# Hybrid RWKV-7 / Mamba-2 / short-convolution block: the first round's norm and logits inside the opening strips, and the key shift ahead of a split

## The reference, cut to what matters

```python
h = rmsnorm(x, norm_w[l]);  p = h @ w_in[l]            # 256 x 2048 times 2048 x (some 17,500)
pa = token_shift(pa, mu)                               # p + mu * (prev - p)
r, k, v, g, dw, da = jnp.split(pa, [...])
log_w = -softplus(-(w0 + tanh(dw) @ w2)) - 0.5         # decay logits: rank 64
decay = exp(-exp(log_w));  a = sigmoid(a0 + da @ a2)   # a second rank 64 product
kk = k * k_k;  k = k * (1.0 + (a - 1.0) * k_a)
kh = kk / maximum(sqrt(sum(kk * kk, axis=-1)), 1e-12)  # norm over each head of 64
# state-space branch: per head, over 256 tokens
dt = softplus(dt + dt_bias);  a_cs = cumsum(dt * a)    # "acs" in the kernel
seg = exp(a_cs[l] - a_cs[s]) where l >= s
```

## Time and profile before

| | |
|---|---|
| median of 3 runs | 1207.26 us (1206.23 to 1207.36) |
| the profiled execution | 1207.42 us |
| its span, first to last instruction | 1205.7 us |
| mean granted TensorE clock | 0.995 of full speed |
| PE busy | 1173.4 us (97%) |
| PEld busy | 1041.9 us (86%) |
| DVE busy | 798.7 us (66%) |
| ACT busy | 572.9 us (48%) |
| POOL busy | 67.8 us (6%) |

### The profile page before, as it was taken

How to read it: one execution, slowest core, us unless ns; L and a number is a source line. 1 busy time by engine, 2 the same in 40 slices (tenths; PEclk the granted TensorE clock), 3 DMA queues, 4 the chain that set the end, 5 groups by cost and what they waited for, 6 DMA issues and landing times.

```text
span 1205.7 us, 23555 instructions
## 1 busy us (share of the span) xinstructions
PE 1173.4 (97%) x8502; PEld 1041.9 (86%) x8502; DVE 798.7 (66%) x1174; ACT 572.9 (48%) x828; POOL 67.8 (6%) x94
## 2 busy tenths in 40 slices
PE   6998999999999999999999999999999999999996
PEld 5997999999899998998989988888888888888885
DVE  4776769678686786876968765754555565546553
ACT  5454446455364554544535444543544444445442
POOL 2001001010010110100101002000000000000000
PEclk9998999999999999999999999999999999999999
DMA  6755635546455354553555536466666666658662
GB/s 167 210 158 132 172 106 158 136 120 172 121 156 153 105 159 137 150 156 104 158 135 139 161 111 204 140 211 208 193 192 190 196 196 193 189 184 283 194 195 95
DMA packets 254747, 197.24 MB, mean 164 GB/s; under 512 B 23943, under 2 KB 207472, under 8 KB 254064
## 3 DMA queue, kind: packets, MB, share of 16 engines
q1 hardware_dynamic: 252228, 195.82, 56.3%
q10 hardware_dynamic: 2476, 0.84, 0.3%
HBM read 193.71 MB, written 2.11 MB: 162 GB/s over the span
## 4 chain that ended last, share of the span: by engine, by line
PE 93%; ACT 2%; DVE 2%; issue 1%; DMA 1%; POOL 0%; SPq 0%; DVEq 0%; ACTq 0%
PE ps L1163 15%; PE ps L1164 13%; PE ps L1165 13%; PE ps L1241 11%; PE ps L1242 11%; PE ps L1243 11%; PE ps L1489 2%; PE ps L1490 2%; PE ps L1491 2%; PE ps L1275 1%; ACT whi L427 1%; PE ps L1358 1%; PE ps L1350 1%; PE ps L1371 1%; DMA o<-in_x 1%
## 5 line engine op out<-in xcount | busy, mean ns | idle before, releaser
L724 DVE TENSOR_TENSOR wlo<-raw,whi 128x1024 fp32r<-128x1024 f32 (+1 forms) x356 | 437.1, 1241 | 241.4 <-ACT whi L427 239.8
L427 ACT ACTIVATE whi<-raw 128x1024 fp32r<-128x1024 f32 (+1 forms) x356 | 372.8, 1054 | 308.4 <-PE ps L1243 182.1
L1163 PE MATMUL ps<-hhi,whi 128*128 128x256 f32 (+1 forms) x1440 | 422.1, 293 | 0.2 <-DVE wlo L724 0.2
L1164 PE MATMUL ps<-hlo,whi 128*128 128x256 f32 (+1 forms) x1440 | 407.4, 283 | 0.0
L1165 PE MATMUL ps<-hhi,wlo 128*128 128x256 f32 (+1 forms) x1440 | 407.2, 283 | 0.0
L1163 PEld LDWEIGHTS ps<-hhi,whi 128*128 128x128 f32 (+1 forms) x1440 | 274.2, 190 | 16.8 <-issue 13.4
L1164 PEld LDWEIGHTS ps<-hlo,whi 128*128 128x128 f32 (+1 forms) x1440 | 274.7, 191 | 0.7
L1165 PEld LDWEIGHTS ps<-hhi,wlo 128*128 128x128 f32 (+1 forms) x1440 | 274.4, 191 | 0.3
L1241 PE MATMUL ps<-whi,hhi 128*128 128x512 f32 x384 | 151.3, 394 | 0.0
L1243 PE MATMUL ps<-whi,hlo 128*128 128x512 f32 x384 | 149.6, 390 | 0.0
L1242 PE MATMUL ps<-wlo,hhi 128*128 128x512 f32 x384 | 149.5, 389 | 0.0
(11 more groups left out here) (270 smaller groups left out, 1137.4 us busy)
## 6 DMA issues: line engine op xcount, KB each, us to landing
raw<-in_w_in SPq DMA_DIRECT2D x548, 256.0 KB, 3.1
raw<-in_w_branch SPq DMA_DIRECT2D x96, 256.0 KB, 3.7
raw<-in_w_out SPq DMA_DIRECT2D x64, 256.0 KB, 3.6
o<-in_x SPq DMA_DIRECT2D x4, 1024.0 KB, 6.8
acb<-acs_rows SPq DMA_DIRECT2D x8, 256.0 KB, 3.4
out_y<-lots SPq DMA_DIRECT2D x3, 512.0 KB, 4.6
lots<-in_final_norm_w SPq DMA_DIRECT2D x1, 1024.0 KB, 10.2
lots<-ad SPq DMA_DIRECT2D x32, 8.0 KB
```

Source lines behind the costliest of these rows:

```text
L427: sc.activation(whi[:, slot, :, 0:width], raw[:, slot, :, 0:width], ACT.Copy).then_inc(hi_done, 1)
L724: tt(wlo[:, slot, :, 0:width], raw[:, slot, :, 0:width], whi[:, slot, :, 0:width].bitcast(F32), ALU.subtract).then_inc(lo_done, 1)
L1163: mm(dst, a, khi, start=first, stop=False)
L1164: mm(dst, a, klo, start=False, stop=False)
```

## The change

- **TensorE:** the transposes of the decay rows and time steps and `norm_and_logits(0)` move from behind the opening into it, after chunk 25. The transposes go to bank `E` instead of `B`, and TensorE no longer waits for ScalarE's copy before the norm.
- **VectorE:** `shift_k(0)` and `shift(0, 0)` move in front of the split in step c = 25 (chunk 27's); `kk_floor(0)`, `kk_recip(0)` and `decays(0)` in front of the split in step c = 27 (chunk 29's).
- **ScalarE:** the copy `dat` follows the split in step c = 26. In step c = 27, in front of the split, it waits for the store of the decay rows, issues their first load itself, and does `kk_root(0)` and `half_logits(0)`.
- **SyncE:** the wait for that store and the first load of the decay rows are gone.
- **Loop, VectorE:** `shift_k(j + 1)` moves from t = 32, behind that step's split, to t = 31, in front of it.

The definitions of the helpers move up with their first use and are the same; they are left out of the diff here.

```diff
@@ SyncE @@
-            sp.wait_ge(s["acs_st"], 16)
-            load_acs(0)
             with sp.Fori(0, CT - 1) as j:
                 main(j, False)
@@ ScalarE @@
             for c in range(PRE):
                 n = c + AHEAD
+                if c == 27:
+
+                    act.wait_ge(s["acs_st"], 16)
+                    act.dma_start(acb[:].rearrange("p e t -> p (e t)"), acs_d[0:1, :].broadcast_to([P, 2 * T])
+                                  ).then_inc(s["acb_in"], 16)
+                    kk_root(0)
+                    half_logits(0)
                 if n > 2:
                     split_hi(n, n % RING, n // RING + 1, P + 16 if n < 4 else CW, first=n < RING)
+                if c == 26:
+                    act.wait_ge(s["dt_tr"], 1)
+                    sc.activation(dat[:].rearrange("p w b h -> p (w b h)"), E[:, 0:64], ACT.Copy).then_inc(s["dat_ok"], 1)
                 if c == 4:
...
-            act.wait_ge(s["dt_tr"], 1)
-            sc.activation(dat[:].rearrange("p w b h -> p (w b h)"), B[:, 0:64], ACT.Copy).then_inc(s["dat_ok"], 1)
...
-            kk_root(0)
-            half_logits(0)
@@ VectorE @@
             for c in range(PRE):
                 n = c + AHEAD
+                if c == 25:
+                    shift_k(0)
+                    shift(0, 0)
+                if c == 27:
+                    kk_floor(0)
+                    kk_recip(0)
+                    decays(0)
                 if n > 2:
                     split_lo(n, n % RING, P + 16 if n < 4 else CW)
...
-            shift_k(0)
-            shift(0, 0)
-            kk_floor(0)
-            kk_recip(0)
-            decays(0)
...
-                    if t == 32 and not last:
+                    if t == 31 and not last:
                         shift_k(j + 1)
@@ TensorE @@
-            pe.wait_ge(s["acs_ok"], 1)
-            pe.wait_ge(s["scm_ok"], 4)
-            for w, src in enumerate((acs[:], dts[:, 5, :])):
-                for b in range(2):
-                    op = tr(B[:, (2 * w + b) * 16:(2 * w + b + 1) * 16], src[:, b * P:(b + 1) * P], ident[0:16, 0:16])
-            op.then_inc(s["dt_tr"], 1)
-            pe.wait_ge(s["dat_ok"], 1)
-            pe.wait_ge(s["lr_ok"], 1)
-            pe.wait_ge(s["const_o"], 1)
...
+                if c == 25:
+
+                    pe.wait_ge(s["acs_ok"], 1)
+                    pe.wait_ge(s["scm_ok"], 4)
+                    for w, src in enumerate((acs[:], dts[:, 5, :])):
+                        for b in range(2):
+                            op = tr(E[:, (2 * w + b) * 16:(2 * w + b + 1) * 16], src[:, b * P:(b + 1) * P], ident[0:16, 0:16])
+                    op.then_inc(s["dt_tr"], 1)
+                    pe.wait_ge(s["lr_ok"], 1)
+                    pe.wait_ge(s["const_o"], 1)
+                    norm_and_logits(0)
...
-            norm_and_logits(0)
```

More of the change, by code:

```diff
@@ L454, in _, with kk_root, half_logits @@
             act.wait_ge(s["prm_d"], 1)
+            def kk_root(j):
+                act.wait_ge(s["kk_max"], j + 1)
+                sc.activation(knrm, ksq, ACT.Sqrt).then_inc(s["kk_rt"], 1)
+            def half_logits(j):
+                act.wait_ge(s["lora_mm"], j + 1)
+                sc.activation(tanhs[:, 0, :], A[:, 0:T], ACT.Tanh, scale=0.5, bias=halfb[:, bass.ds(j, 1)])
+                sc.activation(tanhs[:, 1, :], C[:, 0:T], ACT.Tanh, scale=0.5,
+                              bias=halfb[:, bass.ds(j + CT, 1)]).then_inc(s["tanh_wa"], 1)
             for c in range(PRE):
                 n = c + AHEAD
+                if c == 27:
[4 more added lines that the diff above has]
+                    half_logits(0)
                 if n > 2:
                     split_hi(n, n % RING, n // RING + 1, P + 16 if n < 4 else CW, first=n < RING)
+                if c == 26:
+                    act.wait_ge(s["dt_tr"], 1)
+                    sc.activation(dat[:].rearrange("p w b h -> p (w b h)"), E[:, 0:64], ACT.Copy).then_inc(s["dat_ok"], 1)
                 if c == 4:
@@ L749, in _, with shift, shift_k, kk_floor @@
             ts(dskh[:], dsk[:], 0.5, None, ALU.mult).then_inc(s["prm_d"], 1)
+            def shift(j, w):
+                dve.wait_ge(tile_out, PRE_TILES + j * ITER_TILES - 3 + ORDER[w])
+                stt(sh[:, w, :], pq[:, w, 0:T], prm[:, bass.ds(j + (MU + w * CT), 1)], qq[:, w, :], ALU.mult, ALU.add
+                    ).then_inc(s["shifted"], 1)
+            def shift_k(j):
+                shift(j, 1)
+                dve.wait_ge(s["shifted"], j * 4 + 1)
+                ts(kk, sh[:, 1, :], prm[:, bass.ds(j + KK, 1)], None, ALU.mult).then_inc(s["kk_ok"], 1)
+            def kk_floor(j):
+                dve.wait_ge(s["kk_mm"], j + 1)
+                ts(ksq, B[:, 0:T], 1e-24, None, ALU.max).then_inc(s["kk_max"], 1)
+            def kk_recip(j):
+                dve.wait_ge(s["kk_rt"], j + 1)
+                v.reciprocal(krin, knrm).then_inc(s["kk_rin"], 1)
+            def decays(j):
+                dve.wait_ge(s["tanh_wa"], j + 1)
+                ts(sga, tanhs, 0.5, 0.5, ALU.mult, ALU.add).then_inc(s["sig_wa"], 1)
+                dve.wait_ge(s["sig_wa"], j + 1)
+                v.tensor_tensor_scan(ls, restart[:], sga[:, 0, :], 0.0, ALU.mult, ALU.add).then_inc(s["cum"], 1)
             for c in range(PRE):
                 n = c + AHEAD
+                if c == 25:
[5 more added lines that the diff above has]
+                    decays(0)
                 if n > 2:
@@ L794, in _ @@
                         tt(scm[:, g, :], ps[:, 4 + g, 0:384], causal[:], ALU.mult).then_inc(s["scm_ok"], 1)
[L796 to L822, removed]
             def gate_split(n, i, y):
@@ L1178, in half_chunk, with norm_and_logits @@
                     op.then_inc(chunk_used, 1)
+            def norm_and_logits(j):
+                pe.wait_ge(s["kk_sq"], j + 1)
+                mm(B[:, 0:T], head1[:], ksq, start=True, stop=True).then_inc(s["kk_mm"], 1)
+                pe.wait_ge(lora_in, j * 32 + 32)
+                mm(A[:, 0:T], lorat[0:64, 0, :], lr[0:64, :], start=True, stop=True)
+                mm(C[:, 0:T], lorat[64:128, 1, :], lr[64:128, :], start=True, stop=True).then_inc(s["lora_mm"], 1)
             x_by_channel(0, 8)
```

## The result

The changed kernel takes 1192.2 us (median of 4 runs, 1191.8 to 1193.5) against 1207.06 us before: a ratio of 0.988, 95% interval 0.9863 to 0.9897, that is 14.9 us or 1.2% less. Forecast were 1193.9 us and a range of 1192.8 to 1197.8. A second timing, with a later set of runs, gave 1192.6 against 1207.7 (0.9876, 0.9861 to 0.9891).

A forecast was written before the change was run, and what follows sets the result against it. TensorE, busy 97%, was taken as the bound, with time to win only in its waits and low clock. Opening 7.6 plus loop 5.8 made 13.4 us, giving 1193.9 us; own range 1192.9 to 1195.2, 8-in-10 range 1192.8 to 1197.8.

The forecast's parts named there:

- The opening, 7.6 us: Norm and logits inside the opening's strips: shorter idle wait 3.7, norm at full clock 1.0, faster round 1 2.9 us.
- the stop: TensorE's 3.88 us idle wait before the first norm, for GpSimd's square of the keys; falls to 0.2, gain 3.7 us.
- the cold norm: First norm to round 1's first product: 2.27 us at low clock, 1.26 at full clock, gain 1.0 us.
- the wait I kept for the square: Opening: TensorE's new wait for GpSimd's square of the keys, 0 to 0.5 us, taken as 0.2.
- The first round: Round 1's excess of 2.90 us over round 2, from half clock and waits at lines 1320 and 1292, all goes.
- The chain to the keys: Opening, norm to scaled keys on VectorE: done at 110.7 us, 1.3 us before TensorE needs them at 112.0.
- I count nothing for it: SyncE's loads of chunks 28 and 29, no longer behind the store's wait: in time even unmoved, so no gain.
- if it is late after all, at least the clock's 1.6 comes back: Round 1: should the scaled keys be late, 1.6 us of the 2.9 us gain still comes from the clock.
- The loop, 7 x 0.83 = 5.8 us: Key shift in front of the split in seven rounds: TensorE's wait at the norm goes, 0.83 us a round.
- VectorE's 0.90 us keeps the distance: Loop: all VectorE's later work moves forward by 0.90 us, so the chain to the next scaled keys keeps its distance.
- The late opening chain: First rival: floor, root, tanh and decays over 1.3 us later than summed, round 1 keeps its waits; 1195.2 to 1197, chance 0.12.
- the second one: Second rival: GpSimd's square goes first, VectorE's split waits 0.61 us each round, loop worth 2.0 us; 1197.7, chance 0.09.

## Why the prediction was right in kind and too small

**The opening, 7.6 us: right in sum.** The first products of the two executions start 0.28 us apart (17.55 and 17.83). With that, the norm of round 2 comes 181.41 - 173.24 + 0.28 = 8.45 us earlier, 0.86 of it its own stall: 7.6. By its terms: the stop and the cold norm give 4.9 instead of 4.7, because the wait I kept for the square, 0.2, was none. The first round gives 2.7 instead of 2.9: I had all of line 1320's wait go, and 0.4 us stayed (24.78 against 24.38), since it depends on the small transfers too. The chain to the keys was summed to within 0.1 us, and the run with the norm a chunk later confirms its room.

**SyncE, "I count nothing for it": wrong, and hidden by the sum.** Put back, wait and load cost 3 us; alone in the old order their removal gives 3.6. I checked whether chunk 28 would be in time for TensorE. I should have asked what else stands behind its split on ScalarE. The sum held by luck: I had laid out the head of round 1 as if nothing held ScalarE there, which is true only with this edit. A fallback of mine fails as well, "if it is late after all, at least the clock's 1.6 comes back": in the run with the loop's edit alone the clock came back early and the keys took the time, and with the load alone on ScalarE the clock fell later instead.

**The loop, 7 x 0.83 = 5.8 us: the step that failed.** I bounded a round's gain by the stall, "between the counted 0.70 and the full 0.98 - 0.12 = 0.86". It is mis-sized: a round gives 0.97, the term 6.8. With the transfers out of the way a round falls from 77.27 to 76.30, 0.97 us. The stall is 0.86 of it. The other 0.11 is the restart: a norm whose square is already there takes 1.16 us to the next product, one that was waited for 1.26 (1.15 to 1.16 and 1.26 to 1.27 in every round from the second on). The weights of the norm itself point at the cause, weights that are not loaded ahead through a stop: they are loaded 0.12 us ahead of it where nothing is waited for (173.12 and 173.24 above), and only with it behind a stop, in the kernel before:

```profile
181.41 0.30 PEld L1212 LDWEIGHTS ps<-lots,head 128*128 128x128 f32 x2 [0.90 <-POOL lots L366]
```

7 x 0.97 = 6.8, and the loop's edit alone measured 6.8. The sentence that VectorE's 0.90 us keeps the distance held, and mattered: without it 0.4 us of each round goes back.

**What was in no term: about 0.6 us.** The waits at line 1320 of rounds 2 to 7, up to 0.2 us each, were not seen as waits, since the list of waits shows only that of round 1. They depend on when the small transfers land: with these first, they are gone in both orders. "Late" fell from 0.72 to 0.14 between the two profiles, and 7.6 + 6.8 + 0.6 makes 15.0. In the six profiles of kernels with the changed opening and the old order of transfers it runs from 0.03 to 0.70, so whether the change lowers it for a reason or by chance is left open. With the small transfers first in both kernels the change is worth 1205.07 - 1191.18 = 13.9 us; by the medians about 1 us of the 14.9 depends on when these transfers land.

**The rivals.** The late opening chain did not come (1.5 us of room), nor did the second one: in the loop the split went first. In the opening GpSimd went first and VectorE's splits lost 0.4 us, inside the room. The Trainium skill (SBUF — State Buffer, "Who interferes with whom") has it that the two share one pair of ports under an exclusive lock, and that the order of issue decides who blocks. The trace agrees to within 0.15 us, with both orders in the changed kernel. In the loop the split had 1.06 of its 1.22 us left when the square started, and the square took 1.53 us, 0.92 more than alone. In the opening the square had 0.55 us left when the splits started, and they took 2.77 us, 0.43 more than alone. The range was too narrow below: its lower end took 0.5 for the runs, 0.2 for the opening's wait and 7 x 0.03 for the loop off the forecast, with no allowance for a term larger than the stall.

## What to carry to other kernels

A stop of the bounding engine costs more than its idle time: the first instructions behind it are not prepared, 0.1 us each time here, and the clock was half from the norm on for 5.6 us behind the stop of 3.88 us, and for some 3 us behind that of 2.33. What the clock gives back counts only where nothing else is late. When work moves past a queue's wait, ask of every in-order engine what stands behind the instruction that is held, not only whether the held one is in time. A list that shows a wait once may hide a smaller one in every round; comparing the same distance from round to round finds it.

## What the runs showed of the hardware

With small transfers (8 KB) issued behind 512 KB of weights on the same queue, the work that waits for them started with a spread of 0.25 us from round to round (the solve, 10.64 to 10.89 us after the transposes in rounds 2 to 7 of the kernel before), and with them issued in front with none that could be seen (10.10 us in each of the same rounds). Behind stops of TensorE of 3.88 and 2.33 us the granted clock was 0.50 for a time, and behind those of 1.3 us and less it stayed at 1.00 (the run with load and wait on SyncE, and that with the norm after chunk 26). How long it stays low varies: 3.5 us from the norm on in the run with the loop's edit alone, 5.6 in the kernel before, with the same opening. ScalarE's table load took 1.28 us and the instruction behind it started at its end (99.76 + 1.28 = 101.04, square root at 101.05).
